# Expert activations in 512-column products into both halves of a bank, summed on VectorE, with two buffers for the value rows

## The reference, cut to what matters

```python
def peer_ffn(h, w_q, sub_keys, expert_u, expert_v):
    ...
    gate = jax.nn.softmax(top, axis=-1)
    def chunk(args):
        hc, ec, gc = args
        u = expert_u[ec]
        act = jax.nn.gelu(jnp.einsum('td,thkd->thk', hc, u), approximate=False)
        return jnp.einsum('thk,thkd->td', gc * act, expert_v[ec])
```

## Time and profile before

| | us |
|---|---|
| median of three executions | 3043.43 (3042.71 to 3046.54) |
| the profiled execution | 3045.64 |
| its span, from first to last instruction | 3043.9 |
| expert loop of layer 0, within the span | 404.6 to 1068.9 |
| expert loop of layer 1, within the span | 1447.8 to 2077.6 |

### The profile page before, as it was taken

How to read it: one execution, slowest core, us unless ns; L and a number is a source line. 1 busy time by engine, 2 the same in 40 slices (tenths; PEclk the granted TensorE clock), 3 DMA queues, 4 the chain that set the end, 5 groups by cost and what they waited for, 6 DMA issues and landing times.

```text
span 3043.9 us, 49161 instructions
## 1 busy us (share of the span) xinstructions
PE 2950.1 (97%) x17378; PEld 2563.1 (84%) x17378; DVE 1965.7 (65%) x3626; ACT 1302.8 (43%) x2098; POOL 274.5 (9%) x398
## 2 busy tenths in 40 slices
PE   8899999999999999999999999998999999999999
PEld 4686989999999876877999999998977988878897
DVE  4769966777777633898666666666556655555664
ACT  1245844444444412575444444444443433534433
POOL 0026700000000000573000000000000000000000
PEclk9899999999999998999999999999999999999999
DMA  8542256666666641403555655554334454424454
GB/s 325 197 157 84 78 186 235 232 223 231 231 228 228 205 154 56 167 8 118 193 188 184 200 188 195 188 197 175 125 114 169 174 180 171 151 111 157 155 180 152
DMA packets 130815, 524.41 MB, mean 172 GB/s; under 512 B 17981, under 2 KB 28093, under 8 KB 108025
## 3 DMA queue, kind: packets, MB, share of 16 engines
q1 hardware_dynamic: 120648, 508.13, 48.3%
q10 hardware_dynamic: 10034, 14.52, 1.4%
HBM read 519.44 MB, written 3.16 MB: 172 GB/s over the span
## 4 chain that ended last, share of the span: by engine, by line
PE 86%; DVE 6%; ACT 4%; issue 1%; DMA 1%; DVEq 1%; ACTq 0%; POOL 0%; SPq 0%
PE acc L1385 23%; PE prob_ps L1373 22%; PE acc L1009 7%; PE acc L1597 6%; PE acc L1610 6%; PE acc L994 3%; PE acc L968 2%; PE acc L1355 2%; PE acc L1544 2%; PE turn_ps L1117 2%; PE prob_ps L1336 2%; PE acc L1569 1%; PE acc L947 1%; PE acc L1091 1%; PE acc L1248 1%
## 5 line engine op out<-in xcount | busy, mean ns | idle before, releaser
L1373 PEld LDWEIGHTS prob_ps<-hTr,utr 128*128 128x128 f32 x5472 | 686.3, 191 | 24.5 <-issue 7.9
L1373 PE MATMUL prob_ps<-hTr,utr 128*128 128x256 f32 x5472 | 697.1, 284 | 1.4 <-issue 1.3
L1385 PE MATMUL acc<-vr,wtr 128*128 128x512 f32 x2736 | 663.7, 391 | 0.1
L1385 PEld LDWEIGHTS acc<-vr,wtr 128*128 128x128 f32 x2736 | 499.3, 188 | 94.9 <-issue 0.5
L2767 DVE TENSOR_TENSOR vr<-slab,vr 128x1024 fp32r<-128x1024 f32 x228 | 279.5, 1226 | 367.5 <-ACT vr L2030 367.5
L2030 ACT CAST vr<-slab 128x1024 fp32r<-128x1024 f32 x228 | 239.4, 1050 | 524.2 <-PE acc L1385 524.2
L2742 DVE TENSOR_TENSOR utr<-slab,utr 128x1024 fp32r<-128x1024 f32 x228 | 277.9, 1219 | 13.2 <-ACT utr L1997 13.2
L2296 POOL TENSOR_TENSOR small<-small 128x1 f32<-128x1 f32 (+4 forms) x29 | 26.2, 903 | 2617.8 <-DVE small L2359 1414.8
L1997 ACT CAST utr<-slab 128x1024 fp32r<-128x1024 f32 x228 | 238.8, 1047 | 16.4 <-DMA slab<-in_peer_u 10.5
L3018 DVE TENSOR_TENSOR slab_lo<-slab,w_hi 128x2048 fp32r<-128x2048 f32 x64 | 143.8, 2288 | 123.5 <-ACT w_hi L2262 123.5
L2262 ACT CAST w_hi<-slab 128x2048 fp32r<-128x2048 f32 x64 | 119.3, 1907 | 158.7 <-DMA slab<-in_pack_b 151.2
(11 more groups left out here) (309 smaller groups left out, 4419.1 us busy)
## 6 DMA issues: line engine op xcount, KB each, us to landing
slab<-in_pack_b SPq DMA_DIRECT2D x132, 1024.0 KB, 4.9
slab<-in_peer_v SPq DMA_DIRECT2D x256, 512.0 KB, 3.5
slab<-in_peer_u SPq DMA_DIRECT2D x244, 512.0 KB, 4.5
arena<-in_pack_a SPq DMA_DIRECT2D x84, 512.0 KB, 4.7
slab<-in_pack_a SPq DMA_DIRECT2D x40, 1024.0 KB, 7.0
arena<-in_peer_u SPq DMA_DIRECT2D x6, 1024.0 KB, 15.4
slab<-in_pack_b SPq DMA_DIRECT2D x4, 832.0 KB, 5.7
arena<-in_pack_a SPq DMA_DIRECT2D x2, 1024.0 KB, 18.4
```

The costliest lines, as they stand in the source:

```text
L1373: ins = pe.matmul(prob_ps[:, m % 2, 0:S], utr[:, m % 2, uh, k * P:k * P + P], hTr[:, hh, k, :], start=(k == 0 and n == 0), stop=(k == KD - ...
L1385: ins = pe.matmul(y_ps[:, t, n, :], wtr[:, m % 2, wh, t * P:t * P + P], v[:, vh, n * 512:n * 512 + 512], start=first and k == 0, stop=last ...
```

## The change

A's products are regrouped. For each of the eight feature slices, the high part of the table is now multiplied by the high and the low part of the activations in one product of 512 columns, whose two results of 256 columns lie in the two halves of the bank; the low part of the table is multiplied by the high part as before and added to the first half. So A has 16 products (8 of 512 columns, 8 of 256). DVE adds the two halves in a new operation, `halves_summed`, a reduction over pairs of elements that lie 256 columns apart in PSUM, into `ga`; it stands ahead of u_low in DVE's order. gelu reads `ga` and writes it in place. The value rows get a second buffer, `vr_odd`, and v_high(i) waits for C(i - 2) in place of C(i - 1). `early_at` moves into the memory region that the second buffer shares with it.

```diff
-                        pe.wait_ge(*gelu_done.at("a", l, i - 1 - EARLY[l]))
+                        pe.wait_ge(*summed.at("a", l, i - 1 - EARLY[l]))
...
                     for k in range(KD):
-                        for n, (uh, hh) in enumerate(HALVES):
-                            ins = pe.matmul(prob_ps[:, m % 2, 0:S], utr[:, m % 2, uh, k * P:k * P + P], hTr[:, hh, k, :],
-                                            start=(k == 0 and n == 0), stop=(k == KD - 1 and n == 2))
+                        for uh in ((0, 1) if k < KD - 1 else (1, 0)):
+                            u = utr[:, m % 2, uh, k * P:k * P + P]
+                            if uh:
+                                ins = pe.matmul(prob_ps[:, m % 2, 0:S], u, hTr[:, 0, k, :], start=False, stop=False)
+                            else:
+                                ins = pe.matmul(prob_ps[:, m % 2, :].rearrange("p (h s) -> p h s", h=2), u, hTr[:, :, k, :],
+                                                start=(k == 0), stop=(k == KD - 1))
...
                 def gelu(i, m):
-                    act.wait_ge(*am_full.at("a", l, i + 1 - EARLY[l]))
-                    if not (isinstance(i, int) and i < 2):
-
-                        act.wait_ge(*wt_ready.at("a", l, i - 1))
-                    act.activation(ga[:, m % 2, :], prob_ps[:, m % 2, 0:S], ACT.Gelu).then_inc(gelu_done.sem, 1)
+                    act.wait_ge(*summed.at("a", l, i + 1 - EARLY[l]))
+                    act.activation(ga[:, m % 2, :], ga[:, m % 2, :], ACT.Gelu).then_inc(gelu_done.sem, 1)
...
-                    if not isinstance(i, int) or i >= EARLY[l]:
+                    if isinstance(i, int) and i == EARLY[l]:
                         act.wait_ge(*v_used.at("a", l, i))
+                    elif not isinstance(i, int) or i > EARLY[l]:
+                        act.wait_ge(*v_used.at("a", l, i - 1))
...
+                def halves_summed(i, m):
+
+                    dve.wait_ge(*am_full.at("a", l, i + 1 - EARLY[l]))
+                    dve.tensor_reduce(ga[:, m % 2, :], prob_ps[:, m % 2, :].rearrange("p (h s) -> p s h", h=2), X, ALU.add)\
+                        .then_inc(summed.sem, 1)
...
                         for j in range(8):
                             i = it * 8 + (PLAIN + 3 + j)
+                            halves_summed(i, (3 + j) % 4)
                             u_low(i + 1, j)
                             weighted(i, (3 + j) % 4)
                             if j < 4:
```

More of the change, by code:

```diff
@@ L316, in two_blocks @@
         gelu_done = Signal(sem("gelu_done"), a=NKEYS - EARLY[0])
+        summed = Signal(sem("summed"), a=NKEYS - EARLY[0])
         wt_ready = Signal(sem("wt_ready"), a=NKEYS)
@@ L365, in two_blocks @@
         small = sb("small", [P, 896])
-        early_at = sb("early_at", [P, max(EARLY), S])
         with ExitStack() as first:
@@ L370, in two_blocks @@
                                (("arena", [P, ARENA]), ("slab", [P, 2, 4096]), ("hT", [P, KD, S])))
+            early_at = first.enter_context(nc.sbuf_tensor("early_at", [P, max(EARLY), S], F32))
         with ExitStack() as second:
@@ L380, in two_blocks @@
             vr = half("vr", [P, 2, D])
+            vr_odd = half("vr_odd", [P, 2, D])
         expert_u = slab[:, 0, 0:2 * D].rearrange("p (q d) -> p q d", q=PLACES)
@@ L407, in v_landed, with v_place @@
             return v_in[m % 2].at("a", l, place + 1 - lent(l, first, m % 2))
-        def v_place(l, i):
+        def v_place(l, i, m):
             if not isinstance(i, int) or i >= EARLY[l] - 1:
-                return vr[:]
+                return vr_odd[:] if m % 2 and not (isinstance(i, int) and i < EARLY[l]) else vr[:]
             return utr[:, 0] if i % 2 else utr[:, 1]
@@ L1380, in combine @@
                     pe.wait_ge(*(last_v_lo.at("a", l, 1) if last else v_lo.at("a", l, i + 1)))
-                    v = last_v if last else v_place(l, i)
+                    v = last_v if last else v_place(l, i, m)
                     for t in range(T):
@@ L2016, in gelu @@
                 def gelu(i, m):
-                    act.wait_ge(*am_full.at("a", l, i + 1 - EARLY[l]))
-                    if not (isinstance(i, int) and i < 2):
-                        act.wait_ge(*wt_ready.at("a", l, i - 1))
-                    act.activation(ga[:, m % 2, :], prob_ps[:, m % 2, 0:S], ACT.Gelu).then_inc(gelu_done.sem, 1)
+                    act.wait_ge(*summed.at("a", l, i + 1 - EARLY[l]))
+                    act.activation(ga[:, m % 2, :], ga[:, m % 2, :], ACT.Gelu).then_inc(gelu_done.sem, 1)
                 def v_high(i, m, place):
                     act.wait_ge(*v_landed(l, i, m, place))
-                    if not isinstance(i, int) or i >= EARLY[l]:
+                    if isinstance(i, int) and i == EARLY[l]:
                         act.wait_ge(*v_used.at("a", l, i))
+                    elif not isinstance(i, int) or i > EARLY[l]:
+                        act.wait_ge(*v_used.at("a", l, i - 1))
                     elif 2 <= i < EARLY[l] - 1:
                         act.wait_ge(*v_used.at("a", l, i - 1))
-                    act.copy(v_place(l, i)[:, 0], v_raw(l, i, m)).then_inc(v_hi.sem, 1)
+                    act.copy(v_place(l, i, m)[:, 0], v_raw(l, i, m)).then_inc(v_hi.sem, 1)
                 act.wait_ge(*htr_lo.at("a", l, 1))
@@ L2765, in v_low @@
                     dve.wait_ge(*v_hi.at("a", l, i + 1))
-                    v_hl = v_place(l, i)
+                    v_hl = v_place(l, i, m)
                     dve.tensor_tensor(v_hl[:, 1], v_raw(l, i, m), v_hl[:, 0].bitcast(F32), ALU.subtract)\
@@ L2775, in _ @@
                 for i in range(EARLY[l], EARLY[l] + 3):
+                    halves_summed(i, i)
                     u_low(i + 1, i + 1)
@@ L2780, in four @@
                     for j in range(4):
+                        halves_summed(first + j, (3 + j) % 4)
                         u_low(first + (1 + j), j)
@@ L2810, in _ @@
                     .then_inc(last_v_lo.sem, 1)
+                halves_summed(NKEYS - 1, 3)
                 weighted(NKEYS - 1, 3)
```

## The result

The kernel after takes 3057.62 us (median of 9 executions), the kernel before 3046.22 in the same comparison: a ratio of 1.0043, with a 95% interval of [1.0034, 1.0052]. That is slower by 0.43%, where no difference was forecast (3045.2).

What follows compares the result with a forecast made beforehand. PE, busy 97% of the span, bounds the kernel, with DVE deciding the ada_piece blocks. Terms -21.3 + 20.5 + 3.8 - 1.4 + 0.2 = +1.8 us on the profiled 3045.64 gave a median of 3045.2, range 3035 to 3058.

Steps and rivals of the forecast that it cites:

- A's products: In A, each of 8 merged pairs saves 11.7 ns, over 228 blocks -21.3 us; ends nothing and -24.3.
- the groups: Twelve groups of four ada_piece blocks in layer 0: DVE's longer queue makes PE wait, +20.5 us; ends +15 and +27.
- the slow sum: Rival: DVE's sum of pairs 1 KB apart in PSUM is slower than a plain read; 3057 or 3070 us, chance 0.17.
- start of each loop: The second A waits for u_low, which waits for the sum: 1.9 us late, +3.8 for two layers.
- loads on ACT's queue: Near layer 0's end, PE's 1.32 us wait behind ACT's transfers goes as v_high runs earlier: -1.4 us.
- end of each loop: Before the last C, 0.5 us of cover for a sum and handover of 0.74: +0.2 us in all.
- the plain blocks: 180 blocks without ada_piece: DVE fits the sum in before PE needs its results, so they keep the whole gain.
- DVE keeps up: Rival: PE never waits in the ada_piece blocks, 3024.7 us, chance 0.06; a milder form, 3036, chance 0.12.
- The wide product is no cheaper: Rival: in A the 512-column product takes 240 ns, so nothing is gained: +19, 3062 us, chance 0.05.
- a path on DVE some 0.15 us longer: Slower case: DVE's path in the ada_piece blocks is longer than worked out, +8 us, chance 0.08.
- makes this possible: In plain blocks, v_high(i) no longer waiting for C(i-1) was said to let them keep the whole gain.

Runs made afterwards that it cites:

- e9_widths_grouped: The kernel after with A's 16 products reordered to seven wide, eight narrow, one wide; 3057.19 us, ratio 1.004 to the kernel before.
- e5_piece_behind_values: The kernel after with v_low moved ahead of ada_piece on DVE's queue; 3037.87 us, ratio 0.9981 to the kernel before.
- e6_piece_behind_and_spread: The kernel after with v_low ahead of ada_piece and the pieces in blocks 0, 1, 3 and 4 of eight; 3036.58 us, ratio 0.9973 to before.

## Why the prediction was wrong

Its mechanism holds: a gain in A and a loss in the blocks with ada_piece that nearly cancel. Two of its terms were mis-sized, both against the change: A's products by 6.0 us and the groups by 2.6. Where the sum is a small difference of large terms, that was enough to turn no difference into a loss. The measured 3057.62 lies just within the stated range all the same, and that is luck: the range's upper end came from the slow sum (3057), and the sum is not slow.

| term | predicted | in the traces |
|---|---|---|
| A's products | -21.3 | -15.3 (228 x 0.067) |
| groups with ada_piece | +20.5 | +23.1 (12 x 1.93) |
| start of each loop | +3.8 | +3.6 (2 x 1.78: PE waits 1.96 us for the second A, and lost some tenths there before) |
| loads on ACT's queue | -1.4 | -1.5 (a C 7.17 us behind the one before it, now 5.55) |
| end of each loop | +0.2 | +0.9 |
| sum | +1.8 | +10.8; the loops' lengths give +10.4 |

*A's products* are the step that failed most. The forecast took the pace of 512 columns from C, where each product follows one of the same width, and that of the narrow ones from an A where all are narrow. In the new A the widths take turns. e9_widths_grouped shows that this is what was missed: grouped, A takes 2.77 us, a little under the predicted 2.79; in turns 2.81. Its ends (0 and -24.3) enclose what came, but the value taken was too near the good end.

*The groups.* The path was followed correctly, and each predicted distance of C is within 0.2 us (6.17, 5.79, 5.91 and 5.79 predicted; 6.26, 5.81, 6.09 and 5.92 shown, of the group above). The path is 6.05 us long and not 5.97, in the fourth block 6.15. What was left out stands between ada_piece and v_low. The prediction counted 0.08 us there for a drain, and so 1.65 for ada_piece; v_low starts 0.17 us behind its end, and 0.26 in the fourth block, where the kernel has a second drain, so it takes 1.74 and 1.83. In the trace of before, v_low waited for v_high there, so the gap was covered. Also v_low needs 0.15 us to reach PE and not 0.10. The prediction said that each 0.1 us on this path is worth up to 4.8; it counted 2.0 for a gap of this kind, from another place, and it was about 4.6 for all of it.

*The end.* Cover for the last sum was read in layer 1. In layer 0 the last value block lands later, and the sum stands behind the v_low that waits for it.

*Right* were the start (a second A that PE waits 1.96 us for, 1.9 predicted), the loads on ACT's queue, the plain blocks, which keep their gain, and the sum of 0.69 us.

*The rivals.* The slow sum is refuted: 691 ns, as long as DVE's plain copy of 512 elements out of PSUM. So DVE reads pairs 1 KB apart at the pace of neighbours. What the Trainium skill says of matmuls, that patterns that aren't contiguous slow them down (Advanced Engine Details and Errata, PSUM Cachelines), does not show in this operation of DVE. "DVE keeps up" did not come about in the change as made, but its condition was wrongly put: the path from the sum to C need not lose the sum, it can lose ada_piece, and with v_low ahead of it e5_piece_behind_values gets within 3.4 us (12 x 0.28) of no wait at all. "The wide product is no cheaper" is refuted, though 6.0 of its 21.3 us were real. The form that the prediction called a path on DVE some 0.15 us longer (a chance of 0.08) is the one that came true in kind: the path was 0.08 to 0.18 us longer, and cost 2.6 us more than forecast, not 6. That the second buffer "makes this possible" was wrong as well: with one buffer the plain block takes 5.56 us too.

*What stays open:* the profiled execution of after is 1.3 us longer outside the loops than that of before, and in the other kernels this part lies between 4.0 us below that of before (e5_piece_behind_values) and 9.2 us above it (e6_piece_behind_and_spread). From the last C to the end it goes with the granted clock (968.7 us at 0.98 before, 975.1 at 0.97 in e9_widths_grouped), not with any work that the change touches.

## What to carry to other kernels

Before work is moved to an engine that is "70% busy", write down its queue for the fullest block, in order, and ask which operations in it someone waits for; those go first, and work that nobody waits for goes behind them or into a block with room. One moved line was worth 20 us here, more than the change's own gain. A pace is taken from instructions in the same neighbourhood: the same product had another price beside products of another width.

## What the runs showed of the hardware

- A 512-column product costs 228 ns among its like, two of 256 columns 240; in turns, a wide and a narrow one cost 0.351 us together, grouped 0.347: about 3 ns for each change of width (or of what changes with it).
- What follows a drain on DVE does not always start alike. Behind ada_piece's drain the sum starts 0.09 us after ada_piece's end in e6_piece_behind_and_spread (36 times, as at 776.01 above), v_low in the kernel after 0.16 to 0.17 (36 times); behind two drains it is 0.18 and 0.26 (12 times each). Why v_low takes 0.08 more was not tried. The 48 gaps ahead of v_low are 9.2 us in all, on the path that PE waits for.
- A reduction over pairs on DVE has the price of its input (691 ns for 512 elements out of PSUM); neither groups of two nor the distance of 1 KB cost anything.
- After PE had stood idle for 1.96 us or more at the start of layer 1's loop, the granted clock fell from 1.00 to 0.50 in four of seven profiled executions and not in three; it cost about 1.6 us. At the start of layer 0's loop the same idle time stood in all seven, and the clock stayed at 1.00.
